# Even layer's attention scores as three rounded products in 44 of 48 units, and the gated tiles' rounding behind the attention

## The reference, cut to what matters

```python
oa = lax.map(lambda qb: gqa_attend(qb, ka, va), qa_blk)             # half A: all 768 keys
kk = jnp.concatenate([c_bk, lax.dynamic_slice_in_dim(kb_pad, start, band, axis=1)], axis=1)
return gqa_attend(qb, kk, vv, bias, sink)                           # half B: context and a band of 384 keys
...
y_lat = jnp.concatenate([oa * jax.nn.silu(ag), ob * jax.nn.silu(bg)], axis=-1) @ w_out
# gqa_attend:
s = jnp.einsum("bqhgd,bkhd->bhgqk", q, k, preferred_element_type=jnp.float32) * ATTN_SCALE
p = jax.nn.softmax(s, axis=-1)
return jnp.einsum("bhgqk,bkhd->bqhgd", p.astype(v.dtype), v)
```

## Time and profile before

| | us |
|---|---|
| median of 3 runs | 1722.84 |
| lowest and highest | 1711.46, 1722.86 |
| the profiled execution | 1721.06 |
| its span | 1719.7 |
| even attention, first to last score in the trace | 1114 to 1326 |

### The profile page before, as it was taken

How to read it: one execution, slowest core, us unless ns; L and a number is a source line. 1 busy time by engine, 2 the same in 40 slices (tenths; PEclk the granted TensorE clock), 3 DMA queues, 4 the chain that set the end, 5 groups by cost and what they waited for, 6 DMA issues and landing times.

```text
span 1719.7 us, 25709 instructions
## 1 busy us (share of the span) xinstructions
PE 1675.4 (97%) x9968; PEld 1378.1 (80%) x9968; DVE 973.6 (57%) x1980; ACT 740.7 (43%) x1477; POOL 653.6 (38%) x291
## 2 busy tenths in 40 slices
PE   8999999999999999999999999999999999999998
PEld 7889777788888888888878888877777888897776
DVE  4699565542232265555498143565666657985643
ACT  5222355552323454444323443265676235225643
POOL 3866322243334455444466511211113233522241
PEclk9999999999999999999999998999999999999999
DMA  8557212132224313333374311100000532221121
GB/s 246 170 161 197 80 50 62 51 110 86 73 85 140 108 50 110 99 98 98 110 225 140 120 49 54 52 26 26 14 26 2 145 116 80 87 74 44 44 74 50
DMA packets 255159, 156.08 MB, mean 91 GB/s; under 512 B 6017, under 2 KB 251070, under 8 KB 255038
## 3 DMA queue, kind: packets, MB, share of 16 engines
q1 hardware_dynamic: 252238, 147.78, 29.3%
q10 hardware_dynamic: 2800, 6.65, 1.2%
HBM read 152.32 MB, written 2.10 MB: 90 GB/s over the span
## 4 chain that ended last, share of the span: by engine, by line
PE 91%; DVE 5%; ACT 2%; issue 1%; DMA 1%; POOL 1%; DVEq 0%; ACTq 0%
PE ps L814 72%; PE ps L2485 3%; PE ps L2516 3%; PE ps L2499 2%; PE ps L1597 1%; PE ps L1613 1%; DVE mod_sums L1544 1%; PE ps L1559 1%; DVE probsT L2596 1%; PE ps L1605 1%; POOL w_lo L784 1%; PE ps L1235 1%; PE ps L2220 0%; PE ps L2520 0%; PE ps L2315 0%
## 5 line engine op out<-in xcount | busy, mean ns | idle before, releaser
L784 POOL TENSOR_TENSOR w_lo<-w_raw,w_hi 128x1024 fp32r<-128x1024 f32 (+2 forms) x220 | 570.7, 2599 | 855.0 <-ACT w_hi L724 854.8
L814 PE MATMUL ps<-h_hi,w_lo 128*128 128x512 f32 x1088 | 440.0, 404 | 8.0 <-DVE h_lo L1133 2.9
L814 PE MATMUL ps<-h_hi,w_hi 128*128 128x512 f32 x1088 | 427.2, 393 | 0.0
L814 PE MATMUL ps<-h_lo,w_hi 128*128 128x512 f32 x1088 | 426.7, 392 | 0.0
L814 PEld LDWEIGHTS ps<-h_hi,w_lo 128*128 128x128 f32 x1088 | 206.2, 189 | 56.6 <-issue 4.7
L724 ACT ACTIVATE w_hi<-w_raw 128x1024 fp32r<-128x1024 f32 (+1 forms) x220 | 228.8, 1045 | 35.4 <-PE ps L814 20.9
L814 PEld LDWEIGHTS ps<-h_hi,w_hi 128*128 128x128 f32 x1088 | 205.8, 189 | 44.6
L814 PEld LDWEIGHTS ps<-h_lo,w_hi 128*128 128x128 f32 x1088 | 206.4, 190 | 42.4 <-issue 2.2
L2569 ACT ACTIVATE probs<-probs,small 128x512 f32<-128x512 f32 (+3 forms) x128 | 93.7, 732 | 29.0 <-DVE small L2585 28.7
L1544 DVE SCALAR_TENSOR_TENSOR mod_sums<-mod_raw,small,mod_sums 128x256 f32<-128x256 f32 x154 | 98.5, 706 | 0.5
L2596 DVE COPY probsT<-ps 128x256 f32<-128x256 f32 (+3 forms) x128 | 55.0, 430 | 66.8 <-PE ps L2499 66.3
(11 more groups left out here) (439 smaller groups left out, 3282.7 us busy)
## 6 DMA issues: line engine op xcount, KB each, us to landing
w_raw<-in_w_in SPq DMA_DIRECT2D x56, 512.0 KB, 5.4
mod_raw<-in_mod_w SPq DMA_DIRECT2D x24, 1024.0 KB, 5.3
w_raw<-in_w_up SPq DMA_DIRECT2D x44, 512.0 KB, 3.6
w_raw<-in_od_w_in SPq DMA_DIRECT2D x28, 512.0 KB, 3.6
w_raw<-in_ev_w_in SPq DMA_DIRECT2D x20, 512.0 KB, 3.7
w_raw<-in_w_down SPq DMA_DIRECT2D x16, 512.0 KB, 4.2
w_raw<-in_w_mem_kv SPq DMA_DIRECT2D x8, 512.0 KB, 3.8
w_raw<-in_w_attn_branch SPq DMA_DIRECT2D x8, 512.0 KB, 3.8
```

What stands on the lines that cost most here:

```text
L784: POOL.tensor_tensor(wlo[:, p, at:n], raw[:, p, at:n], f(whi[:, p, at:n]), ALU.subtract).then_inc(*chunk_lo.by(c))
L814: ins = PE.matmul(out, l, r, start=first and n == 0, stop=last and n == 2)
```

## The change

1. In 44 units (all of A; in B p = 28 to 47) the scores become three rounded products per part and head: high queries by low keys, low queries by high keys, high by high. `pe_split_scores` does them; units 24 to 27 keep the fp32 scores.
2. The keys of A are split before the attention (`act_high_keys` on ACT, `dve_low_keys` on DVE ahead of the last rotation), those of B at p = 24 and 25 (`act_high_keys_again`, `dve_low_keys_again`). The low keys are written over the keys themselves, the high ones into `early_tiles`.
3. The queries of each unit are split two units ahead: high by ACT ahead of its exponential of p, low by DVE behind the second maximum of p, ahead of the copy for head 1.
4. As `early_tiles` is taken, `EARLY` is 0: all eight gated tiles are rounded in `act_even_out` and subtracted in `dve_even_out`. POOL's and ACT's early share goes.
5. A semaphore (`upper_rows`) is merged into `rows_dve`, with no other effect.

```diff
+    key_high, crossed_high = put("key_high", [P, ALL], F32R), put("crossed_high", [P, ALL], F32R)
+    query_high = [put(f"query_high{n}", [P, P], F32R) for n in range(3)]
+    put = region(GATED_AT + 4 * 3 * ALL)
+    key_low, crossed_low = put("key_low", [P, ALL], F32R), put("crossed_low", [P, ALL], F32R)
+    query_low = {x_: put(f"query_low_{x_}", [P, 4, ALL], F32R) for x_ in "AB"}
...
-    EARLY = 3
+    EARLY, SPLIT_AGAIN = 0, 28
...
-                if i in (5, 6):
-                    for early in ((0, 1), (2,))[i - 5]:
-                        pool_gated_low(early)
...
         act_cross_keys("A")
         next(at)
+        act_high_keys()
         run(at)
...
             next(at)
             dve_rope("B", n)
+        dve_low_keys()
         dve_rope("B", 3)
...
+    def pe_split_scores(x_, p, u):
+        PE.wait_ge(*split_low(p))
+        for off, w, at in u["scores"]:
+            for n, (q, k) in enumerate(u["split"]):
+                for s in range(2):
+                    first = u["at"][s] + off
+                    if (off, s, n) == (512, 0, 0):
+                        PE.wait_ge(*p_scored(x_, p, "own bank"))
+                    ins = PE.matmul(ps[:, first:first + w], q[s * HEAD:(s + 1) * HEAD, :], k[s][s * HEAD:(s + 1) * HEAD, at:at + w],
+                                    start=n == 0, stop=n == 2, skip_group_check=True)
...
+    def act_high_queries(p):
+        if p >= 3:
+            ACTE.wait_ge(*p_scored("E", p - 3))
+        x_, n, at = query_of(p)
+        ACTE.activation(query_high[p % 3][:], qT3[x_][:, n, at:at + P], ACT.Copy).then_inc(*split_high.by(p))
+    def dve_low_queries(p):
+        DVE.wait_ge(*split_high(p))
+        x_, n, at = query_of(p)
+        DVE.tensor_tensor(query_low[x_][:, n, at:at + P], qT3[x_][:, n, at:at + P], f(query_high[p % 3][:]),
+                          ALU.subtract).then_inc(*split_low.by(p))
...
+    def act_high_keys_again(p):
+        if p == 24:
+            ACTE.wait_ge(*p_scored("E", 23))
+            ACTE.activation(key_high[:], kk_["B"][:], ACT.Copy).then_inc(*split_high.by("own keys B"))
+        if p == 25:
+            ACTE.wait_ge(*keys_crossed("B"))
+            ACTE.activation(crossed_high[:], kx_["B"][:], ACT.Copy).then_inc(*split_high.by("crossed keys B"))
...
+    def dve_low_keys():
+        DVE.wait_ge(*split_high("own keys"))
+        DVE.wait_ge(*keys_crossed("A"))
+        DVE.tensor_tensor(key_low[:], kk_["A"][:], f(key_high[:]), ALU.subtract).then_inc(*split_low.by("own keys"))
+        DVE.wait_ge(*split_high("crossed keys"))
+        DVE.tensor_tensor(crossed_low[:], kx_["A"][:], f(crossed_high[:]), ALU.subtract).then_inc(*split_low.by("crossed keys"))
+        dve_low_queries(0)
+        dve_low_queries(1)
...
+                    u["split"] = (qh, kl), (ql, kh), (qh, kh)
...
-            if p >= 31 and (p - 31) % 6 == 0 and (p - 31) // 6 < EARLY:
-                if p == 31:
-                    ACTE.wait_ge(*p_attended("E", 11))
-                act_gated_high((p - 31) // 6)
+        def before(p):
+            act_high_keys_again(p)
+            if p + 2 < 24 or SPLIT_AGAIN <= p + 2 < 48:
+                act_high_queries(p + 2)
...
                 dve_gate(*GATED[i], i)
+            dve_low_keys_again(p)
+            if p + 2 < 24 or SPLIT_AGAIN <= p + 2 < 48:
+                dve_low_queries(p + 2)
...
     def act_even_out():
-        ACTE.wait_ge(*p_attended("E", 23))
-        for i in range(EARLY, len(GATED)):
+        ACTE.wait_ge(*p_scored("E", 47))
+        for i in range(len(GATED)):
+            if i == 3:
+                ACTE.wait_ge(*p_attended("E", 23))
             act_gated_high(i)
```

More of the change, by code:

```diff
@@ L319, in build @@
     put = region(GATED_AT)
+    key_high, crossed_high = put("key_high", [P, ALL], F32R), put("crossed_high", [P, ALL], F32R)
+    query_high = [put(f"query_high{n}", [P, P], F32R) for n in range(3)]
+    put = region(GATED_AT + 4 * 3 * ALL)
+    key_low, crossed_low = put("key_low", [P, ALL], F32R), put("crossed_low", [P, ALL], F32R)
+    put = region(R0 + 4 * DT * CTX)
+    query_low = {x_: put(f"query_low_{x_}", [P, 4, ALL], F32R) for x_ in "AB"}
+    put = region(GATED_AT)
     gated_hl = put("g_hi_lo", [P, DT, 2, ALL], F32R)
     ghi, glo = gated_hl[:, :, 0, :], gated_hl[:, :, 1, :]
-    EARLY = 3
+    EARLY, SPLIT_AGAIN = 0, 28
     put = region(rest)
@@ L498, in build @@
     p_maxed = signal("p_maxed", halves)
+    split_high, split_low = [signal(name, ["own keys", "crossed keys"] + list(range(24)) + ["own keys B", "crossed keys B"] +
+                                     list(range(SPLIT_AGAIN, 48))) for name in ("split_high", "split_low")]
     p_exped = signal("p_exped", halves)
@@ L561, in build @@
     g_silu = signal("g_silu", gated + each("cg", 4))
-    g_prod = signal("g_prod", gated[:6] + [("low", 0), ("low", 1), gated[6], ("low", 2)] + gated[7:])
+    g_prod = signal("g_prod", gated)
     g_hi = signal("g_hi", gated + each("cg", 4))
@@ L584, in build @@
     rows_act = signal("rows_act", (1, 3))
-    rows_dve = signal("rows_dve", (0, 2))
+    rows_dve = signal("rows_dve", ("upper", 0, 2))
     BANK, BEFORE, EMPTIED, holder = {}, {}, {}, {}
@@ L2477, in halves_turned @@
         return rows_, ident[rows_, rows_]
+    def pe_split_scores(x_, p, u):
[8 more added lines that the diff above has]
+                                    start=n == 0, stop=n == 2, skip_group_check=True)
+                    if (off, s, n) == (0, 1, 2) and (x_, p) in wide:
+                        ins.then_inc(*p_scored.by(x_, p, "own bank"))
+        ins.then_inc(*p_scored.by(x_, p))
     def pe_scores(x_, p, u):
+        if "split" in u:
+            pe_split_scores(x_, p, u)
+            return
         for off, w, at in u["scores"]:
@@ L2642, in build, with query_of, act_high_keys, dve_low_keys_again @@
     KEY_BLOCK = (2, 3, 0, 1, 4, 5)
+    def query_of(p):
+        n, i = divmod(p % 24, 6)
+        return "AB"[p // 24], n, (CTX + i * P if i < NB else (i - NB) * P)
+    def act_high_queries(p):
[8 more added lines that the diff above has]
+                          ALU.subtract).then_inc(*split_low.by(p))
+    def act_high_keys():
+        ACTE.activation(key_high[:], kk_["A"][:], ACT.Copy).then_inc(*split_high.by("own keys"))
+        ACTE.wait_ge(*keys_crossed("A"))
+        ACTE.activation(crossed_high[:], kx_["A"][:], ACT.Copy).then_inc(*split_high.by("crossed keys"))
+        act_high_queries(0)
+        act_high_queries(1)
+    def act_high_keys_again(p):
[5 more added lines that the diff above has]
+            ACTE.activation(crossed_high[:], kx_["B"][:], ACT.Copy).then_inc(*split_high.by("crossed keys B"))
+    def dve_low_keys_again(p):
+        if p == 24:
+            DVE.wait_ge(*split_high("own keys B"))
+            DVE.tensor_tensor(key_low[:], kk_["B"][:], f(key_high[:]), ALU.subtract).then_inc(*split_low.by("own keys B"))
+        if p == 25:
+            DVE.wait_ge(*split_high("crossed keys B"))
+            DVE.tensor_tensor(crossed_low[:], kx_["B"][:], f(crossed_high[:]), ALU.subtract).then_inc(
+                *split_low.by("crossed keys B"))
+    def dve_low_keys():
[6 more added lines that the diff above has]
+        dve_low_queries(1)
     def even_pairs(x_):
@@ L2661, in pair @@
                          out=qT3[x_][:, n, at:at + 2 * P] if i % 2 == 0 else None)
+                if x_ == "A" or 24 + len(us) >= SPLIT_AGAIN:
+                    qh, ql = query_high[len(us) % 3], query_low[x_][:, n, at:at + P]
+                    kh, kl = [[(own_ if s == kv else other) for s in range(2)]
+                              for own_, other in ((key_high, crossed_high), (key_low, crossed_low))]
+                    u["split"] = (qh, kl), (ql, kh), (qh, kh)
                 u["bias"] = [band[:, zero * P:(zero + tiles) * P] if x_ == "B" else zero1.to_broadcast([P, tiles * P])] * 2
@@ L2751, in pool_gate_even @@
         POOL.tensor_tensor(attended_tile(i), silu_t[i % 2][:], attended_tile(i), ALU.mult).then_inc(*g_prod.by(*GATED[i]))
-    def pool_gated_low(i):
-        POOL.wait_ge(*g_hi(*GATED[i]))
-        POOL.tensor_tensor(glo[:, i, :], attended_tile(i), f(ghi[:, i, :]), ALU.subtract).then_inc(*g_prod.by("low", i))
     def act_gated_high(i):
@@ L2774, in beside @@
                 act_round(round_after[GATED[(p - 5) // 6]])
-            if p >= 31 and (p - 31) % 6 == 0 and (p - 31) // 6 < EARLY:
-                if p == 31:
-                    ACTE.wait_ge(*p_attended("E", 11))
-                act_gated_high((p - 31) // 6)
-        pairs_ = act_pairs("E", even_units, probs2, probsT2, beside=beside)
+        def before(p):
+            act_high_keys_again(p)
+            if p + 2 < 24 or SPLIT_AGAIN <= p + 2 < 48:
+                act_high_queries(p + 2)
+        pairs_ = act_pairs("E", even_units, probs2, probsT2, before, beside)
         next(pairs_)
@@ L2825, in act_last_out @@
         for h in range(2):
-            ACTE.wait_ge(*(freed_dve("wo3", DT - 1) if h else upper_rows("added")))
```

(3 more changed lines are left out.)

1 line of the change is left out of this document (removed).

## The result

| | before | after |
|---|---|---|
| median of 20 runs each | 1722.19 us | 1724.38 us |
| lowest and highest | 1711.46, 1723.76 | 1719.88, 1730.8 |
| profiled execution, its span | 1721.06, 1719.7 | 1723.33, 1721.9 |

The ratio is 1.0022, with a 95% interval of 1.0012 to 1.0031: between 2.1 and 5.3 us slower, about 3.8; the two medians are 2.2 us apart. The forecast was +4.6 us, at 1727.4.

A forecast was written before the change was run, and what follows sets the result against it. PE, busy 97% of the span, was taken as the bound, with short DVE waits; -3.4 + 0.7 + 0.2 + 2.4 - 0.1 + 3.1 + 1.7 = +4.6 us gave a median of 1727.4 us, range 1713 to 1742.

The forecast's parts named there:

- Scores of A: Half A's 16 wide units: rounded parts at 0.36 us save 0.21 us each, -3.4 us; narrow units count nothing.
- rival 1: Score products: the two heads' halves don't overlap with rounded operands, +36 us, 1759 us; 12%.
- The start: Ahead of half A's first score: DVE's key and query subtractions delay the last rotation, +0.7 us.
- Half B: Half B's rounds: +2.4 us, plus +0.2 for splitting its keys and -0.1 for first-round context scores.
- disputed price t: Half B's middle units: one narrow rounded product per pair of heads, taken as 0.109 us, bounded by 0.065 and 0.215.
- The hold by POOL: Half B, query of p % 6 = 5: POOL's rounding holds DVE's subtraction, +0.65 us in each of three rounds.
- Rival 2: Half B's narrow rounded parts cost the upper bound, 0.215 us per product, +5.7 us, 1733 us; 20%.
- The key switch in B and the first round's context units: Start of half B: splitting the second half's keys, +0.2 us; the first round's remaining context scores, -0.1 us.
- The gap: Behind the attention: PE waits for late gated tile 0 before the output product, +3.1 us; later tiles never late.
- The half clock behind it: Behind the gap: PE's idling halves the granted clock for 3.4 us, +1.7 us.
- Rival 3: At a gate, POOL takes the port ahead of DVE's query subtraction, seven times, +10 us, 1737 us; 7%.
- Rival 4: All open prices at their low ends: -3.6 us, 1719 us, slightly faster than before; 11%.

The follow-up runs named there:

- e7: Changed kernel with a head's three products issued one behind the other instead of the heads in turn; 1725.02 us, ratio 1.0015.
- e4: Changed kernel with the low keys and first two low queries subtracted one rotation earlier; one profile only, start 3.72 us, half A 109.75 us.
- e5: Changed kernel with middle B units' key tiles reordered, giving two parts of 256 keys and one of 128; 1722.38 us, ratio 1.002.
- e3: Changed kernel with the high query of each round's last unit issued ahead of ACT's rounding work; one profile only, half B 110.61 us.
- e1: Kernel before with only the gated tiles all rounded late (EARLY = 0); 1724.59 us, ratio 1.0027.
- e2: Changed kernel with gated tiles 0 to 2 rounded and subtracted in the last three units; 1721.87 us, ratio 1.0006.
- e8: Kernel of e6 with half B left to fp32 scores; 1716.07 us, ratio 0.9962.
- e9: Same kernel as e8, timed again beside e10; 1716.22 us, ratio 0.9964.
- e10: Same kernel as e6, timed again beside e9; 1713.96 us, ratio 0.9962.
- e6: Changed kernel with the edits of e2, e3, e4 and e5 together; 1715.32 us, ratio 0.9984.

## Why the prediction was right, point by point

The total alone says little: the range reached from 1713 to 1742, and a change worth nothing would have lain in it too. 0.65 us of the 3.0 by which 1727.4 was too high is the median of three runs that it started from (1722.84, over 20 runs 1722.19). What bears the prediction out are the single stretches.

**Scores of A** (-3.4 forecast, -3.60 found): 16 wide units at 1.12 to 1.13 instead of 1.35 us, 0.225 each. The narrow units of A gave nothing, as forecast (over each pair of them the times of after and before differ by 0.01 to 0.05 us). The row taken for it, a rounded product on 128 rows, gave the right 0.12 us, and rival 1, the halves one behind the other, is refuted by the pairs starting together and by e7, which took away even the favourable order in the source. I gave that rival 12%, too much: transposes and fp32 products on 64 rows had both shown the overlap.

**The start** (+0.7, found +0.77): in the timeline of after the subtractions begin at 1112.83 and the rotation behind them ends at 1115.65, 0.2 us ahead of the first score at 1115.85. That is 2.8 us, where the steps made 2.9. e4 shows that it was the place in the queue and not the work.

```profile
1112.83 0.95 DVE L2719 TENSOR_TENSOR key_low<-k_A,key_high 128x768 fp32r<-128x768 f32 x1
1113.69 0.95 DVE L2721 TENSOR_TENSOR crossed_low<-k_crossed_A,crossed_high 128x768 fp32r<-128x768 f32 x1
1114.56 0.48 DVE L2685 TENSOR_TENSOR query_low_A<-q_A,query_high 128x128 fp32r<-128x128 f32 x2
1114.97 0.68 DVE L2234 TENSOR_TENSOR rope_turned<-ps,sin_T 128x512 f32<-128x512 f32 x1
```

**Half B** (+2.4 + 0.2 - 0.1 = +2.5, found +2.96). The disputed price t, bounded by 0.065 and 0.215 us, is 0.11 (taken: 0.109), by the timeline and by e5. A split middle unit stands at 1.38 on the chain, the steps had 1.34. The hold by POOL was in the right unit, by the right mechanism, and a little under-sized: 0.65 forecast, 0.75 measured by e3, which makes 0.3 of the missing 0.46 us. The other 0.16 is found in e3, which has no hold, by the distances from one unit's first score to the next: each round's first end unit saves 0.14 as forecast, its two middle units cost 0.43 together (0.50 forecast), the second end unit saves 0.07 (0.14 forecast) and the context units nothing (0.07 forecast). That is 0.07 a round more than forecast, three times, less what the first round of B did not cost (next point). Rival 2 (t = 0.215) is refuted.

**The key switch in B and the first round's context units** (+0.2 and -0.1). Units 24 to 27 have fp32 scores before and after, and only the work on the keys is new there: from the first score of unit 24 to that of unit 28 it is 17.22 us before and 17.30 after. So the switch costs 0.07, and with the two context units behind it the round grows by 0.05, where +0.1 was forecast. The other three rounds grow by 0.96, 0.95 and 1.00.

**The gap** (+3.1, found +3.04; e1 alone +3.04, e2 +0.01). The first late tile takes the times that ACT's and DVE's first late operations had before. Later tiles never made PE wait, as forecast.

**The half clock behind it** (+1.7). Here the forecast was right in the place and wrong in the sum. The gap of 3.16 us has 2.9 us of idle PE. After, e1, e3, e4 and e7 do show a granted clock near half for 3.4 us behind the gap, and it costs 1.2 to 1.4 us there (26.8 to 27.0 instead of 25.6). e5 has the gap and no such stretch (25.48). But after, e1, e4, e5 and e7 lack the one near 1415 us, which before, e3, e8, e9 and e10 have. e2 and e6, which have no gap, lack it too, so that the gap alone doesn't decide it. In the profile of after the end of the program is shorter by 3.1 us for want of it and of half of another near 1630: e1, which lacks only the first, is shorter there by 1.35 us, and e10, which lacks only the second half, by 1.95. Over the runs, the mean granted clock is 0.9906 in after and 0.9904 to 0.9919 in the three groups of before, so within their range. The step that failed is to price a half-clock stretch as an addition: where it appears, others later in the program may stay out, and what decides that is open. Without this term the sum is +2.9, and at equal clock +3.2 was found.

**Rival 3** (POOL ahead of the query's subtraction at a gate) is refuted: of the 44 query subtractions in the timeline of after, 37 take 0.3 us, one 0.73, and the six of 2.2 us are those of p % 6 = 5, none of them at a gate. Of these six the three in A cost nothing, as forecast: e3 shortens them and leaves A at 109.79. **Rival 4** (all prices low) did not come: t, the hold and the gap were all measured at or above the values taken. But a time of 1719 is one that the kernel can be made to give: e10's 1714 lies under it.

Net: what A gains in 16 units (3.6) B loses through narrow parts and one held subtraction (2.96), and what remains is the gap and the start, which come from where tiles and keys are subtracted and not from the rounded products.

## What to carry over

A change may hold a real gain and hide it behind its placing. Price each moved instruction at the place in the queue where it lands: here one tile's rounding, two key subtractions and one small query subtraction, worth 3.0, 0.8 and 2.25 us, together outweighed a gain of 3.6, and each could be put elsewhere for nothing. Before splitting a product into three rounded ones, look at its column counts: 256 columns gained 0.07 us a part and pair of heads, 128 columns lost 0.11, and choosing another order of key tiles turned the one into the other. When single runs spread by 0.7% and the effect is 0.2%, compare stretches between marks in the profile, and times at equal granted clock.

## What the runs showed of the hardware that was not expected

- Products on the two row halves ran at the same time although one stood three places behind the other in the source of the kernel (e7: A 109.92 us against 109.77, pairs 0.01 us apart).
- The product that follows a rounded one of 256 columns starts 0.12 us behind it, the one that follows a rounded one of 128 columns 0.11 us, but only 0.06 behind the first narrow one. Every product has weights of its own, so the weight load may set the 0.11; that was not tried by itself, and transposes, with 128 columns of weights too, follow at 0.065 us a pair.
- Nearly the whole spread of the runs, 1712.5 to 1725.4 us for the kernel before beside e1 to e6, goes with the mean granted clock (0.989 at about 1724, 0.996 at about 1712.6), and after the clock is taken out 0.9 us of scatter is left. In the profiles the loss is made of stretches at half clock, of 3.4, 6.8 or 10.2 us (the last one, at the end of the span, of 6.5 to 9.3). Some recur near the same place in every profile, as those near 1600 and at the end, and some don't.
- The gap of 3.16 us, 2.9 of them with an idle PE, was followed by such a stretch in five profiles of six (not in e5).
